# Block sums of W2 formed in the opening block, between the strips; one job a unit in the first MLP product

## What is computed

```python
hl = _modulate(xl, mod_l[0], mod_l[1])
pl = jnp.split(hl @ w_in[l] + b_in[l], PROJ_SPLITS, axis=-1)      # 1024 -> 5120 columns
ol_h, _, _ = _hgrn_branch(pl[1], pl[2], pl[3], pl[4], pl[5], ...)  # gated linear recurrence, both directions
mix_l = _merge(pl[0], ol_h, pl[6], w_four_proj[l], w_hgrn_proj[l], w_out[l], b_out[l])   # Fourier branch, gates, W_out
xl = _layernorm(DEEPNORM_ALPHA * xl + mod_l[2] * mix_l, ln_post_g[l, 0], ln_post_b[l, 0])
hl2 = _modulate(xl, mod_l[3], mod_l[4])
xl = _layernorm(DEEPNORM_ALPHA * xl + mod_l[5] * _mlp(hl2, w_mlp1[l], b_mlp1[l], w_mlp2[l], b_mlp2[l]), ...)

def _mlp(h, w1, b1, w2, b2):
    return jnp.square(jax.nn.relu(h @ w1 + b1)) @ w2 + b2
```

## Time and profile before

| | us |
|---|---|
| median of 3 runs | 3223.57 |
| the runs | 3222.33 to 3227.64 |
| the profiled execution | 3226.03 |
| its span, first to last instruction | 3224.2 |
| PE busy | 2957.7 (92%) |
| DVE busy | 1853.1 (57%) |
| ACT busy | 1033.3 (32%) |
| POOL busy | 482.0 (15%) |

### The profile page before, as it was taken

How to read it: one execution, slowest core, us unless ns; L and a number is a source line. 1 busy time by engine, 2 the same in 40 slices (tenths; PEclk the granted TensorE clock), 3 DMA queues, 4 the chain that set the end, 5 groups by cost and what they waited for, 6 DMA issues and landing times.

```text
span 3224.2 us, 35999 instructions
## 1 busy us (share of the span) xinstructions
PE 2957.7 (92%) x13816; PEld 2428.7 (75%) x13816; DVE 1853.1 (57%) x2496; ACT 1033.3 (32%) x1676; POOL 482.0 (15%) x628
## 2 busy tenths in 40 slices
PE   6999999999996889989999798897999799989994
PEld 3888888888884678868788576775888688878883
DVE  5831133112222878857766766665777666687667
ACT  2421000111112555542112444444555433313330
POOL 0423011010101222202202200010111000060003
PEclk9999999999999999989999898898999899999997
DMA  6732233333334545448847666776888755545552
GB/s 227 250 116 82 76 104 121 114 113 106 127 112 154 176 132 177 135 140 236 230 158 245 233 203 199 209 249 216 252 266 262 251 211 189 189 160 212 194 184 98
DMA packets 332912, 573.01 MB, mean 178 GB/s; under 512 B 23731, under 2 KB 212419, under 8 KB 326726
## 3 DMA queue, kind: packets, MB, share of 16 engines
q1 hardware_dynamic: 256646, 330.00, 32.1%
q0 software_dynamic: 58128, 200.85, 18.6%
q10 hardware_dynamic: 17968, 39.85, 3.7%
HBM read 371.37 MB, written 199.24 MB: 177 GB/s over the span
## 4 chain that ended last, share of the span: by engine, by line
PE 46%; DMA 9%; DVE 7%; issue 3%; ACT 2%; POOL 1%; SPq 0%; ACTq 0%; DVEq 0%; POOLq 0%
PE mix_bank L1562 5%; PE mix_bank L1563 5%; PE mix_bank L1564 5%; PE mix_bank L1524 4%; PE mix_bank L1525 4%; PE mix_bank L1526 4%; PE mix_bank L2328 3%; DMA tail_cm<-scratch_xn 3%; PE mix_bank L2267 2%; PE mix_bank L130 2%; PE mix_bank L132 2%; PE mix_bank L131 2%; DMA scratch_xn<-tail_cm 1%; PE mix_bank L1469 1%; PE mix_bank L1470 1%
## 5 line engine op out<-in xcount | busy, mean ns | idle before, releaser
L1524 PE MATMUL mix_bank<-tail_oph,tail_wh 128*128 128x512 f32 x896 | 363.7, 406 | 80.8 <-DVE tail_e L1113 46.2
L130 PE MATMUL head_bank<-head_hTh,head_wh 128*128 128x512 f32 x1024 | 400.9, 392 | 3.1 <-DVE head_hTl L547 2.3
L131 PE MATMUL head_bank<-head_hTl,head_wh 128*128 128x512 f32 x1024 | 398.6, 389 | 0.0
L132 PE MATMUL head_bank<-head_hTh,head_wl 128*128 128x512 f32 x1024 | 398.5, 389 | 0.0
L1562 PE MATMUL mix_bank<-tail_oph,tail_ah 128*128 128x512 f32 x896 | 353.9, 395 | 36.9 <-DVE tail_sum L1183 14.7
L1525 PE MATMUL mix_bank<-tail_opl,tail_wh 128*128 128x512 f32 x896 | 360.2, 402 | 0.0
L1526 PE MATMUL mix_bank<-tail_oph,tail_wl 128*128 128x512 f32 x896 | 359.8, 402 | 0.0
L555 DVE CAST head_wh<-head_raw 128x1024 fp32r<-128x1024 f32 x64 | 44.6, 697 | 543.5 <-PE head_bank L132 414.5
L1563 PE MATMUL mix_bank<-tail_opl,tail_ah 128*128 128x512 f32 x896 | 352.6, 393 | 0.0
L1564 PE MATMUL mix_bank<-tail_oph,tail_al 128*128 128x512 f32 x896 | 352.4, 393 | 0.0
L309 ACT ACTIVATE head_stage<-head_bank,all_b_in_col 128x512 f32<-128x512 f32 (+1 forms) x136 | 91.4, 677 | 590.8 <-PE head_bank L132 567.3
(11 more groups left out here) (274 smaller groups left out, 5477.6 us busy)
## 6 DMA issues: line engine op xcount, KB each, us to landing
tail_a<-scratch_a SPq DMA_DIRECT2D x112, 512.0 KB, 3.2
head_raw<-in_w_in SPq DMA_DIRECT2D x64, 512.0 KB, 4.1
scratch_proj<-head_stage POOLq DMA_DIRECT2D x128, 256.0 KB, 2.7
tail_raw<-in_w SPq DMA_DIRECT2D x64, 512.0 KB, 5.8
scratch_a<-tail_e SPq DMA_DIRECT2D x128, 256.0 KB, 6.3
tail_op<-scratch_w2t SPq DMA_DIRECT2D x28, 1024.0 KB, 5.7
scratch_a<-tail_sm SPq DMA_DIRECT2D x96, 256.0 KB, 8.8
tail_op<-in_w SPq DMA_DIRECT2D x21, 1024.0 KB, 5.7
```

Of the source, the lines that this page charges most:

```text
L130: nc.tensor.matmul(out, wh, xh, start=(k == 0), stop=False)
L131: nc.tensor.matmul(out, wh, xl, start=False, stop=False)
L132: last = nc.tensor.matmul(out, wl, xh, start=False, stop=(k == k_tiles - 1))
L1524: nc.tensor.matmul(out[:], wh[p % 7][:, k, :], oph[i][:, k, :], start=(k == 0 and i in (0, 1, 3)), stop=False, skip_group_check=True)
```

## The change

The sixteen W2 jobs move from the tail to the opening block. There SP loads the block into `x[:, 0]` at steps 13, 15, ... 43, behind the step's own load of W_in; one step later DVE forms the sums right behind `weights(r)`, and SP stores them behind the next load of W_in. The first block waits until x has left its buffer, and ACT waits for the last stores before it reuses it. In the tail the work list is four token sums (units 2 to 5) and then sixteen row jobs (units 6 to 14 and 17 to 23), one after product 5 of a unit. The waits of the down stage's loads for W2 sums go.

```diff
+        MIX0, NMIX = 13, 16
+        mcm = x[:, 0].rearrange("p s n -> p (s n)")
+        mct = x[:, 1, 0, :]
+        def block_job(r):
+            return (r - MIX0) // 2 if r >= MIX0 and (r - MIX0) % 2 == 0 and (r - MIX0) // 2 < NMIX else None
...
@@ sync, behind the load of step r
+                q = block_job(r)
+                if q is not None:
+                    if q:
+                        sp.wait_ge(blk_out, 32 * q)
+                    else:
+                        sp.wait_ge(xT, 4 * NG)
+                        for i in range(2):
+                            sp.wait_ge(st_x[2 + i], 16 * 3 + 16 * (1 - i))
+                    for n in range(2):
+                        sp.dma_start(x[:, 0, :, n * 512:(n + 1) * 512],
+                                     d["w2"][q * 2 * P:(q + 1) * 2 * P, n * 512:(n + 1) * 512].rearrange("(i p) n -> p i n", p=P)).then_inc(ld_blk, 16)
+                q = block_job(r - 1)
+                if q is not None:
+                    dst = d["w2t"][q // 4, :, :, q % 4]
+                    sp.wait_ge(blk_s, 4 * q + 3)
+                    sp.dma_start(dst[0:2].rearrange("o p n -> p o n"), mct.rearrange("p (o n) -> p o n", o=2)).then_inc(blk_out, 16)
+                    sp.wait_ge(blk_s, 4 * q + 4)
+                    sp.dma_start(dst[2:4].rearrange("o p n -> p o n"), mcm[:, 512:1536].rearrange("p (o n) -> p o n", o=2)).then_inc(blk_out, 16)
...
@@ vector
+            def block_sums(r):
+                q = block_job(r - 1)
+                if q is None:
+                    return
...
+                dve.wait_ge(ld_blk, 32 * (q + 1))
+                nc.vector.tensor_tensor(t1, b12, b11, ALU.subtract).then_inc(blk_s, 1)
...
             for n in range(SL, NS1):
                 weights(n + 1)
+                block_sums(n + 1)
             dve.wait_ge(st_b, 32)
             for n in range(NU_):
                 weights(NS1 + n + 1)
+                block_sums(NS1 + n + 1)
                 if n % 4 == 3:
...
@@ tail
-    MIX = 8 + UH
+    MIX = 8
...
-    SPLIT = 2
-    WORK = [("row", n) for n in range(NTILE)] + [("mix", q) for q in range(4, MIX)]
-    SLOTS = [(u, i) for u in range(SPLIT, SPLIT + NTILE // 2) for i in (1, 5)] + [(u, 5) for u in range(10, UH - 1)] + [(UH - 2, 1)] + [
-        (u, 5) for u in range(UH + 1, NU - 1)]
-    WORK_AT = dict(zip(sorted(SLOTS), WORK))
+    WORK = [("mix", q) for q in range(4, MIX)] + [("row", n) for n in range(NTILE)]
+    WORK_AT = dict(zip([(u, 5) for u in range(2, NU - 1) if u not in (UH - 1, UH)], WORK))
...
-                sp.wait_ge(*mix_out(11 + 4 * b))
...
             if r == 0:
                 sp.wait_ge(st_left, LEFT0 + 16 * NTILE)
-                sp.wait_ge(*mix_out(MIX - 1))
...
             if n == 0:
-                pool.wait_ge(*mix_out(2))
-                pool.wait_ge(z_s, NTILE)
-                for s in range(2):
-                    pool.wait_ge(st_hf[s], 16 * 4 * 4)
+                pool.wait_ge(*mix_out(MIX - 1))
                 pool.dma_start(cm[0][:, 1, :], d["res"][0, :].partition_broadcast(P)).then_inc(ld_cm[0], 16)
                 pool.dma_start(ag[:], d["res"][1, :].partition_broadcast(P)).then_inc(ld_cm[0], 16)
```

39 lines of the change are left out of this document (21 added, 18 removed).

## The result

| | before | after |
|---|---|---|
| median of 4 runs, us | 3224.66 | 3174.53 |
| the runs | 3222.33 to 3227.64 | 3173.36 to 3179.22 |
| ratio, 95% interval | | 0.9847 (0.9830 to 0.9864) |
| span of the profiled execution | 3224.2 | 3172.3 |

The change gains 50 us of the 80 that were forecast (3144). The time lies inside the range, and near its slow end. The stretches of the two spans, one profiled execution each, show where the rest went. Each boundary is the start of an instruction: DVE's cast of step 46 of W_in for the opening block, the first matmul of a product for the up and the down stage.

A forecast was written before the change was run, and what follows sets the result against it. PE, busy 92%, gains only where it waits, through DVE, for the row buffer's trips, and in slow clock behind waits. Gains of 85.1 less costs of 6 give 79.1: 3226.0 to 3146.9, less 2.5 is 3144; range 3123 to 3184.

The forecast's parts named there:

- Row jobs spread: Up stage, units 3 to 9: with one row job a unit each takes 19.04 us, a gain of 48.5 us.
- unit 14: Up stage: its two W2 jobs go and it falls from 27.64 to 19.04 us, a gain of 8.6 us.
- the trips are not the cause: Units 3 to 9: traffic and DVE's load make them slow, so half the loss stays; 3168 us, chance 0.05.
- First row job: Up stage: its row and two broadcasts load behind the last token sums, a cost of 1 us.
- Turn: Turn to the down stage: SP need not stand 6.0 us for W2 sums, gain 6 us, bounds 0 and 10.
- Units 15 and 16: Change of tokens: of 32.0 us lost there, 10 stay and 22 are gained; bounds 8 and 32.
- DVE bounds the change of tokens: Units 15 and 16: DVE's own work fills both, only 8 of the 32 us go; 3158 us, chance 0.14.
- Opening block, DVE's sums: Sixteen jobs of 4 x 0.69 us, 44 us on DVE, hide behind PE's work; cost 0.
- Opening block, SP's queue: Two-step loop of W2 loads, sums and stores takes 16.9 us against PE's 16.3 in six-tile pairs; cost 5, ends 0 and 17.
- One of my signs of being wrong: Opening block: PE showing gaps at pair after pair of six tiles would show the forecast wrong.
- The Trainium skill's estimate of the loop: Opening block: two DMAs together take 4.4 us, the loop 14.0, no cost; the sum would be 3139.
- the loop starves the pairs: Opening block: W_in lands only behind 1 MB of W2, the loop takes 19.2 us or more; 3156 us, chance 0.13.

The follow-up runs named there:

- experiment 6: Two row jobs a unit in units 6 to 13, against a kernel with the change's work, two W2 block buffers, later stores and sums behind the moves: 3213.5 us.
- experiment 7: Seven token-operand subtractions replaced by copies, against the change with two block buffers, later W2 stores and sums behind moves: units 15 and 16 took 55.1 us against 60.0.
- experiment 3: The change with its 64 opening-block subtractions but without the W2 loads (except the first block) and stores, sums unused in the down stage: 3165.3 us, 0.9803.
- experiment 8: Three of seven token-operand subtractions moved to POOL, against the change with two block buffers, later W2 stores and sums behind moves: 3159.4 us, 0.9796.
- experiment 9: Row-job loads and stores cut in three, against the change with two block buffers, later W2 stores and sums behind moves: POOL's DRAIN 2.91 us, end 36.7 us.
- experiment 5: Three kernels with parts of a reordering on the change; in-place sums in two block buffers alone: step 46 cast at 607.4 us, against 601.5 in the change.

## Why the prediction was right, and where it was off

The bound was read rightly: waits behind one buffer, and a clock that falls behind them. The time fell inside the range because the range took in the slow bounds of two terms at once; the forecast itself missed by 30 us. Term by term, forecast and then measured from the stretches above:

- **Row jobs spread, 48.5, and unit 14, 8.6: right**, 57.1 of 57.1. Both came from subtracting the length of a free unit from windows of slow ones, and experiment 6 shows the cause. The rival that the trips are not the cause falls.
- **First row job, cost 1:** measured 0, unit 6 takes 19.04.
- **Turn, 6:** measured 5.1. SP no longer stands for W2 sums, and ACT's wait fell from 7.3 to 1.3 us.
- **Units 15 and 16, 22: off**, measured 7.6, the low bound of 8; the same work in eight other kernels took 59.9 to 61.9, which would make it 8 to 10. The step that failed is the sentence that the casts waited because SP issued their loads late behind DVE's stall. With the stall gone DVE still waits 14.4 us for ACT's casts (15.2 before), and ACT's casts had waited only 6.0 us for loads before, 4.8 after. I had worked out that DVE has 39 us of work in 38 us, and then let only 10 of the 32 us rest on it. The time of the rival "DVE bounds the change of tokens" is what came. Its mechanism is shown in part: DVE's work is on the path (experiment 7), but what else holds these units is open.
- **Opening block, DVE's sums, 0: nearly.** Alone they cost 3.1 us, at one place, ahead of the last six moves (experiment 3); I had named the place, but under the other term.
- **Opening block, SP's queue, 5: off**, measured 15.6 beyond what stood at step 13, with the end of the range at 17 (the 3.1 of DVE's sums are in it). The mechanism is as told, the loop of two steps and PE paying at the first strip behind the pairs. Its size is the term that was mis-sized. From store to store the loop took 15.9 to 16.3 us in the middle of groups (16.9 forecast), but 18.6 to 22.8 in every second place, where POOL stores a group's rows. The mean of the six in groups of six tiles, from the stores of block 9 at 458.09 to those of block 15 at 566.73, is 18.1. PE leaves 16.3, so six of them fall 10.8 us behind, not 3.6. I had weighed the DMA share of the pairs as a mean (0.36), in which these bursts don't show. And I had not seen that moves which come late come in a burst, and then wait for one of four stage buffers (5.24 us), where before they went out at PE's pace. One of my signs of being wrong came in part: PE did wait in the pairs, four times and 4.0 us in all, none over 1.4. The Trainium skill's estimate of the loop from two DMAs ("DMA: Bandwidth & Descriptors", Anatomy of one DMA) was 14.0 us and no cost; the trace disagrees even in the light case, 15.9. The Trainium skill gives that fit for DMAs on GpSimd's path, and these are SP's, so it priced something near and not this. The rival "the loop starves the pairs" is what happened, at 18.1 us a loop in place of its 19.2, with 11 us on top of the 5.
- **Not in the sum:** POOL's closing DRAIN, +3.1 us. The kernels after the change vary from 593.3 to 596.1 in the down stage, so the size of the 1.2 there says little, and the -2.0 in the middle is scatter (1224 to 1233).

The sum of what was measured is -57.1 - 7.6 - 5.1 + 15.9 - 2.0 + 1.2 + 2.9 = -51.8, and the spans differ by 51.9. Against the forecast of -79.1 these are 27 us: 14 are the tokens, 11 the opening block, 3 the end, and the small ones cancel. (The 30 us between the forecast and the median hold 3 more, since the profiled execution stood 2.5 us above the median of the three runs before, and 0.4 below the median after.) I had given each of the first two a rival of its own (3158 and 3156) with a chance near one in seven, and didn't price both at once: 3144 + 14 + 12 = 3170.

## What to carry to other kernels

A store that waits for another engine makes every load behind it in its queue as late as that engine is: the same DMAs and the same sums cost 15.9 us in one order and nothing in another with a second buffer, and the cure was three small changes of which two, made alone, did not help. To price such a loop, take the landings in the bursts of the other queues and not the mean DMA share, and ask what a late start does to the buffers downstream. Where two rivals are independent, price the case in which both come true.

## What the runs showed of the hardware

- A two-operand operation of DVE that starts while a subtraction of 128x2048 runs on POOL ends 0.55 us behind it: it took 4.55 to 4.88 us in the place of 0.69, three times out of three (experiment 8).
- POOL's closing DRAIN took 2.91, 4.47 or 7.57 us by what its queue had carried, the same to 0.01 us in all kernels with the same DMAs of POOL (experiment 9).
- SP's issue of a DMA, 0.37 us in the pairs of the kernel before, took 3.67 us for two and then 2.81 for one while POOL's stores of rows ran beside the loads of W2 and W_in, and loads of 0.5 MB landed after up to 10.5 and 12.0 us, at medians of 5.7.
- Loads that were issued earlier, while the stores were still running, took longer to land (median 7.5 against 5.7 us), and so did the loads of W_in issued behind them (7.2 against 5.7; experiment 5, one execution).
